# One block of two chains in the first mixer of a hybrid decoder step, in place of two blocks one after the other

## The reference, cut to what matters

```python
h = x @ w_in                      # split into hq, hf, hi, hg | nq, ncmp, nslc, nwin, ngate
f = lb + (1.0 - lb) * sigmoid(hf);  hg_q = silu(hq);  hg_k = 1.0 - f;  hg_lf = log(f)
S, o = hgrn2_chunk(S0, q, k, v, lf)   # gated linear recurrence, 8 heads, 64x64 state
o = o * rsqrt(mean(o * o) + eps) * hg_norm_g * silu(hg_gate)
q_rope = rope(q);  slc_kv, win_kv: rope on the keys      # sparse attention, 8 heads, 2 kv heads
kc = mean over blocks of 32 (cmp keys + pe);  vc = mean over blocks of 32 (cmp values)
```

## Time and profile before

| | us |
|---|---|
| median of 3 runs | 2352.76 |
| lowest, highest | 2347.38, 2353.86 |
| profiled execution, own time | 2354.03 |
| its span | 2352.2 |

### The profile page before, as it was taken

How to read it: one execution, slowest core, us unless ns; L and a number is a source line. 1 busy time by engine, 2 the same in 40 slices (tenths; PEclk the granted TensorE clock), 3 DMA queues, 4 the chain that set the end, 5 groups by cost and what they waited for, 6 DMA issues and landing times.

```text
span 2352.2 us, 19944 instructions
## 1 busy us (share of the span) xinstructions
PE 1775.9 (75%) x6115; PEld 849.8 (36%) x6115; DVE 1459.7 (62%) x3290; ACT 559.0 (24%) x1747; POOL 717.3 (30%) x612
## 2 busy tenths in 40 slices
PE   7998677947787788586977695779764878657676
PEld 5565354622232322232433242334211545423221
DVE  1553523568877755776589537755954556457966
ACT  1010420022232221332223213322221212122222
POOL 0032000034444432343345423333331222133343
PEclk9985668979999999898999898889987777778987
DMA  6232007069999999899999998999999888899997
GB/s 217 92 94 54 1 35 216 1 240 421 421 420 421 416 407 411 353 410 413 419 421 382 419 397 322 362 364 390 403 383 356 308 320 333 323 373 390 387 378 295
DMA packets 152163, 750.89 MB, mean 319 GB/s; under 512 B 22092, under 2 KB 54744, under 8 KB 72056
## 3 DMA queue, kind: packets, MB, share of 16 engines
q0 software_dynamic: 84480, 608.21, 64.1%
q1 hardware_dynamic: 67576, 141.41, 16.5%
HBM read 743.96 MB, written 5.60 MB: 319 GB/s over the span
## 4 chain that ended last, share of the span: by engine, by line
DMA 26%; PE 23%; DVE 19%; issue 6%; ACT 2%; PEldq 1%; SPq 1%; POOL 1%; PEld 1%; DVEq 1%; ACTq 0%; POOLq 0%
DMA uv<-in_experts_dram,slots 16%; PE ps L2455 12%; DVE uv L2363 6%; PE ps L583 4%; PE ps L1106 2%; DMA sample_cache<-in_odd_w_in_dram 2%; PE ps L1078 2%; DMA sample_w<-in_peer_w_q_dram 1%; DMA last_w<-in_odd_w_in_dram 1%; PEldq L2491 1%; DVE route_s L2198 1%; DVE acc L2377 1%; ACT diag L2431 1%; DVE route_ef L2234 1%; DMA out_dil_p_dram<-dil_val 1%
## 5 line engine op out<-in xcount | busy, mean ns | idle before, releaser
L2455 PE MATMUL ps<-uv,diag 128*128 128x512 f32 (+1 forms) x1880 | 990.1, 669 | 270.8 <-ACT diag L2431 208.5
L2345 POOL DMA_INDIRECT uv<-in_experts_dram,slots x576 | 685.0, 1189 | 1447.1 <-PE ps L2455 1031.2
L2363 DVE CUSTOM_DVE_ANT_0 uv<-uv,x 128x1024 f32<-128x1024 f32 x512 | 622.9, 1225 | 316.0 <-DMA uv<-in_experts_dram,slots 254.2
L2455 PEld LDWEIGHTS ps<-uv,diag 128*128 128x128 f32 (+1 forms) x1880 | 354.9, 201 | 823.6 <-issue 478.6
L2409 ACT ACTIVATE gelu<-dot 128x2 f32<-128x2 f32 x288 | 58.6, 203 | 1107.4 <-DVE dot L2363 1107.1
L2431 ACT ACTIVATE diag<-const,wgt 128x128 f32<-128x128 f32 (+1 forms) x470 | 165.0, 387 | 9.4
L2418 ACT ACTIVATE wgt<-gate,gelu 128x1 f32<-128x1 f32 x576 | 138.0, 287 | 42.4 <-SPq L2561 15.5
L2377 DVE SCALAR_TENSOR_TENSOR acc<-uv,wgt,acc 128x1024 f32<-128x1024 f32 x101 | 129.3, 1280 | 0.9 <-ACT wgt L2418 0.8
L2363 DVE CUSTOM_DVE_ANT_0 uv<-uv,xs 128x1024 f32<-128x1024 f32 x64 | 78.2, 1227 | 74.9 <-DMA uv<-in_experts_dram,slots 73.4
L583 PE MATMUL ps<-last_w,xT 128*128 128x512 f32 x160 | 77.3, 629 | 9.8 <-DMA last_w<-in_odd_w_in_dram 7.6
L583 PE MATMUL ps<-first_w,xT 128*128 128x512 f32 x160 | 74.5, 603 | 3.1 <-DMA first_w<-in_odd_w_in_dram 3.0
(11 more groups left out here) (427 smaller groups left out, 1789.7 us busy)
## 6 DMA issues: line engine op xcount, KB each, us to landing
sample_cache<-in_cache_dil_kv_dram SPq DMA_DIRECT2D x64, 256.0 KB, 7.7
cache<-in_even_w_in_dram SPq DMA_DIRECT2D x12, 1024.0 KB, 6.9
first_w<-in_odd_w_in_dram SPq DMA_DIRECT2D x12, 1024.0 KB, 10.9
last_w<-in_odd_w_in_dram SPq DMA_DIRECT2D x12, 1024.0 KB, 11.9
sample_cache<-in_odd_w_in_dram SPq DMA_DIRECT2D x12, 1024.0 KB, 17.3
uv<-in_experts_dram,slots POOLq DMA_INDIRECT x576, 11.0
uv<-in_peer_w_q_dram SPq DMA_DIRECT2D x8, 1024.0 KB, 12.5
first_w<-in_peer_w_q_dram SPq DMA_DIRECT2D x8, 1024.0 KB, 10.5
```

Of the source, the lines that this page charges most:

```text
L2345: self.k.nc.gpsimd.indirect_dma_start(out=self.uv[:, s % RING, :], out_offset=None, in_=self.table, in_offset=bass.IndirectOffsetOnAxis(ap ...
L2363: ins = nc.vector.tensor_tensor_reduce(self.uv[:, s % RING, 0:D], self.uv[:, s % RING, 0:D], x, 1.0, 0.0, ALU.mult, ALU.add, self.dot[:, g ...
L2455: last = nc.tensor.matmul(k.bank(c)[0:m, :], self.diag[:, s % RING, 0:m], self.uv[:, s % RING, D + 512 * c:D + 512 * (c + 1)], start=(j == ...
```

## The change

The two calls become one, with six stages in the first chain and four in the second. The lengths are changed: in the first chain gate 14, levels 80, keys 5, outputs 35, norm 22, turning of the result 5; in the second rows 100, rotation 18, pooling 12, turning 14. `cache_loads` is no stage any more: its gathers are POOL's only work in the block. The cmp gathers wait for nothing in the block; the slc gathers on POOL and the window loads on SP wait for the end mark of `rows`. For that `wbuf` is moved to the slc and win part of the cache memory, and the buffer of the earlier column projection to the cmp part. The spread values go to `work` in place of `k.xT`, which `rows` still reads. SP's list is the norm weight, the weight loads of `rows`, the window loads, the stores of the states, and last the stores that wait for the rotation. Steps that read `h` wait for the projection jobs that write it (`wait_jobs`).

```diff
-def together(k, name, chains, loads=(), await_stores=False):
+def together(k, name, chains, loads=(), await_stores=False, gathers=()):
-    ended = [k.sem(name, f"chain{i}_ended") for i in range(len(chains))]
+    ended = k.chain_ended = [k.sem(name, f"chain{i}_ended") for i in range(len(chains))]
...
         def _(pool):
-            for stages in chains:
-                for stage in stages:
-                    if "gpsimd" in stage.parts:
-                        stage.parts["gpsimd"](pool)
+            for stage in gathers:
+                stage.parts["gpsimd"](pool)
...
+    def wait_jobs(eng, n):
+        eng.wait_ge(v_out, (n + 1) // 2)
+        eng.wait_ge(s_out, n // 2)
+    stage.wait_jobs = wait_jobs
...
-        together(k, "hg_rows", ([lasting(gate_stage, 16), lasting(level_stage, 80), lasting(keys_turned, 6)], [lasting(rows, 102)]),
-                 [(rows, "sync")])
...
-        v_b_of = lambda hd: k.xT[0:NS, 4 + 2 * (hd % 2):6 + 2 * (hd % 2), :].rearrange("p c n -> p (c n)")[:, 0:DEC_B * HD]            .rearrange("p (b v) -> p b v", v=HD)
+        v_b_of = lambda hd: work[0:NS, :, :].rearrange("p c n -> p (c n)")[:, DEC_B * HD * (hd % 2):DEC_B * HD * (hd % 2 + 1)]\
+            .rearrange("p (b v) -> p b v", v=HD)
...
+                if hd == 0:
+                    rows.wait_jobs(dve, 3)
...
+            rows.wait_jobs(pe, 3)
...
+            rows.wait_jobs(act, 6)
...
+            rows.wait_jobs(dve, 6)
...
-        chain = [lasting(out_stage, 30), lasting(norm_stage, 26), lasting(turn_cat, 5)]
-        together(k, "hg_nsa", (chain, [cache_loads] + beside), [(cache_loads, "sync"), (norm_stage, "sync")] + [(stage, "sync") for stage in beside if "sync" in stage.parts]
-                 + [(out_stage, "sync")], True)
+        chain = [lasting(gate_stage, 14), lasting(level_stage, 80), lasting(keys_turned, 5), lasting(out_stage, 35),
+                 lasting(norm_stage, 22), lasting(turn_cat, 5)]
+        cache_loads.rows_ended = lambda eng: eng.wait_ge(k.chain_ended[1], 3)
+        together(k, "hg_nsa", (chain, [lasting(rows, 100)] + beside), [(norm_stage, "sync"), (rows, "sync"), (cache_loads, "sync"),
+                 (out_stage, "sync")] + [(stage, "sync") for stage in beside if "sync" in stage.parts], True, (cache_loads,))
...
         def _(sp):
+            stage.rows_ended(sp)
...
             for n in ("cmp", "slc"):
+                if n == "slc":
+                    stage.rows_ended(pool)
...
-        return [lasting(turned_round, 16), lasting(pool_stage, 20), lasting(turn, 16)]
+        return [lasting(turned_round, 18), lasting(pool_stage, 12), lasting(turn, 14)]
...
-            wbuf = caches.all[:, 0:8192].rearrange("p (s c n) -> p s c n", s=4, c=4)
-            wbuf_T = caches.all[:, 8192:12288].rearrange("p (s c n) -> p s c n", s=2, c=8)
+            wbuf = caches.all[:, 4096:12288].rearrange("p (s c n) -> p s c n", s=4, c=4)
+            wbuf_T = caches.all[:, 0:4096].rearrange("p (s c n) -> p s c n", s=2, c=8)
```

## The result

The changed kernel took 2334.13 us, median of 19 executions (2319.93 to 2358.53); the kernel before, on the same chips, 2345.80 us, median of 19 (2337.15 to 2353.86). The ratio is 0.9948, 95% interval 0.9931 to 0.9964: about 12 us faster. I forecast 2354.4, no change that can be measured, and a range of 2345 to 2361, so the result lies outside the range. The profiled execution has a span of 2334.7 us and its own time of 2336.54.

A forecast was written before the change was run, and what follows sets the result against it. Both blocks were taken as bound by PE's instruction list; -2.8 - 1.4 + 12.6 - 6.8 = +1.6 us on 2354.0 gave 2355.6, and with the median 1.3 us below that execution, 2354.4; range 2345 to 2361.

The forecast's parts named there:

- The clock: 1.4 us gained: Head steps: without the gap ahead, the clock still falls, but 4.6 us after their start instead of 1.8; 1.4 us gained.
- The clock stays up: Rival: all head steps keep the full clock, 22.9 us in place of 31.4, another 8.5 us gained; chance 0.15.
- The sum: All terms up to the block's end: -2.8 - 1.4 + 12.6 - 6.8 = +1.6 us.
- the front: Projection up to the head steps: PE starts these at about 149.0 instead of 151.84, 2.8 us gained.
- the list: PE's work from the head steps' end to the norm's start: 45.9 us in place of 33.3, 12.6 us lost.
- the norm: The norm's own stretch, mainly DVE: 20.6 us in place of 27.4, 6.8 us gained.
- The wait for the keys' input: Projection: the earlier cross product lets PE find its keys 0.9 us earlier.
- the tick of 1.07 us: Row projection: one tick of matmul work, by which DVE's chain behind the cross product begins earlier.
- The order on PE: Ahead of the norm: state products mixed with three pooling rounds and turning groups 1 to 6, then the end mark.
- the side by side state products: Neighbouring state products without a wait run two at once; all eight take 14.6 us against 14.8, 0.2 gained.
- the new wait: Ahead of turning's first group, PE waits for pooling's end mark and so for DVE; 3.2 us lost.
- Turning and the norm in single file: Rival: turning's groups don't overlap the norm's first five steps; 7.2 us more, +8.8 in all; chance 0.13.

The follow-up runs named there:

- `after_seam`: Changed kernel with two unread 512-column matmuls added on PE between the row projection and the first head step; 2333.34 us, 0.9934 of before.
- `gap_short`: Changed kernel with PE waiting ahead of the first head step for DVE to clear 288 columns, a pause of 1.77 us; 2347.97 us, 1.0022 of before.
- `norm_ahead`: Changed kernel with pooling's rounds put behind the last state product, so no pooling or turning precedes the norm on PE; 2331.32 us, 0.9948 of before.
- `norm_ahead_again`: `norm_ahead` run once more, unaltered; 2326.46 us, 0.9924 of before.
- `after_again`: The changed kernel run once more, unaltered; 2335.67 us, 0.9952 of before.
- `norm_ahead_seam`: `norm_ahead` unaltered, a third profile; despite its label no matmuls were added; 2332.05 us, 0.9933 of before.
- `norm_ahead_hot`: `norm_ahead` with unread bf16 matmuls added on PE behind state products, between pooling's items and in turning; 2339.02 us, 0.9938 of before.

## Why the prediction was wrong

**The step that failed** is in "The clock: 1.4 us gained": "They also wouldn't hold it". From head steps that didn't raise a low clock, and from one fall in a stretch of still smaller matmuls, I inferred that the head steps lose a full one a few us behind their start. They needn't. Not raising and not holding are different things: the same instructions ran 19.3 us at the full clock in 11 profiles, and some 32 us without bringing it back in 9 others. The fall near 1976.7 was a poor stand-in: it shows that matmuls of 8 columns can lose a full clock while PE is busy, as the state products do here, but not that the head steps do.

The Trainium skill (TensorE: Matmul & The Clock Gate, the section on HAM oscillation) has idle gaps as what brings the clock down. The gaps that it speaks of are longer than any pause here, so the pauses put back and the pauses filled agree with its direction and go further: 1.77 us was enough. The 4 profiles that lost the clock with 0.3 us of pause, and the falls in the state products with PE busy, show that the gap alone doesn't settle it.

**The rival that came nearest** was "The clock stays up", at a chance of 0.15 and with 22.9 us for the head steps. Its size was off as well: I took the first step's 2.86 us as the full speed, though part of it lay behind the fall. At the full clock a step is 2.4 us, 19.3 in all. Of the work behind it I had half at the full clock; in the changed kernel it falls about 1 us into the state products (0.52 from 168.5 on, in the next to last window).

**The sum, where the clock falls as I forecast,** was nearly right. The three other profiles of the changed kernel show it, 200.6 to 201.05 us to attention against 198.5 and 199.1 of before: 1.5 to 2.6 us more, where I summed to 1.6. In part that is luck: the front and the clock gave 1.4 to 1.9 us less than forecast, the list and the norm were 0.9 us better. (The kernel before came out at 2345.80 in the comparison, 7 us below the 2352.76 that I started from; that moves the forecast time, and not the step that failed.) By terms:

- The front: 2.8 forecast; from the projection's first matmul to the head steps 1.7 (101.50 less 99.79). The wait for the keys' input did shrink by 0.9, from 1.11 to 0.17 (143.80). But ahead of the cross product, which now comes one tick earlier, PE stands 1.05 us (139.07), a wait that the sum lacks; the profile names no releaser, and DVE is done with its step ahead of it at 138.97. Nor does the tick of 1.07 us come out of the figures given for it: (145.65 - 142.01 - 1.11) / 2 is 1.27.
- The clock in its own terms: 1.4 forecast. Where it fell, the head steps took 0.6 to 1.1 us less than before (32.82 against 31.76 to 32.23), as it fell 2.6 to 3.1 us behind their start, and not 4.6.
- The list: 45.9 forecast, 45.6 measured. The order on PE, the side by side state products and the new wait (3.2 forecast, 3.07) came as written.
- The norm: 20.6 forecast, 20.0 measured, with its tail: 9.8 us without PE, where the forecast had six steps of 8.6 us.

Where the clock holds, as in the profile of the result, the difference to before is 13.5 of the head steps, 1.7 of the front and 7.4 of the norm gained, and 11.4 of the list lost: 11.2 us, the whole of what the stages show.

**Turning and the norm in single file,** the rival of the other side: no. The norm's stretch was shorter than forecast.

**What stays open.** First, what decides, with 0.3 us of pause, whether the clock falls; the records don't show it, and the kernels don't differ there. Nor is it tested whether the filled pauses kept the clock because PE wasn't idle, or because the work in them was matmuls of 512 columns: all four fillings were of these. Second, how often the timed executions of the changed kernel lose it. One of its 4 profiles kept it, yet its two medians (2334.13, 2335.67) lie only 0.8 and 2.3 us above that of `after_seam`, 3 to 4 us by the ratios, where an execution with the fall would be some 14 us longer. So most timed ones probably do keep it. Their records have the granted clock only as a mean over the whole execution, and that doesn't tell: it is 0.856 in the profile of `after_seam`, which kept the clock, and 0.865 in that of `gap_short`, which lost it. Third, how much of `norm_ahead`'s gain of 8.5 us ahead of attention reaches the end: 6.3 us by the two versions with filled seams (0.9907 against 0.9934), 6.6 by `norm_ahead_again` and `after_again`, which ran side by side (0.9924 against 0.9952; by their medians 9.2), and nothing by `norm_ahead` against the changed kernel (both 0.9948) or by `norm_ahead_seam` against `after_seam` (0.9933 and 0.9934). The intervals overlap in each pair. The rest of the kernel varies from 2084 to 2110 us between profiles without an edit there.

## What to carry to other kernels

Ahead of a stretch of light matmuls, look at the pause on PE and at the clock just behind it: a full clock may last through all of the stretch, and if it is lost at the entry it isn't given back. Two matmuls that nothing reads, put into that pause, were worth as much here as a rebuilt schedule, and they are a cheap test of whether the pause matters. Compare stages from landmark to landmark over several profiles: one execution can fall into either case, and a gain of 8 us drowns in a rest that varies by 26.

## What the chip showed unexpectedly

- The same kernel, with the same order and the same pauses, has head steps of 19.3 us in one execution and 32 in another; the choice is made within 3.1 us of their start.
- Light matmuls (64 columns, PE never idle) can hold a full clock for 19.3 us, and did in 11 profiles, but didn't raise a low one in 32, in any of 9.
- 1.8 to 2.8 us of matmuls with 512 columns in the pause kept the clock in 4 of 4 profiles, even where DVE was late by 3 us; bf16 ones with 64 weight columns among the state products and pooling did not stop its fall at 170.5 in the one profile of `norm_ahead_hot`.
